# Strassen-like input projection: signs turned so that weight sums only add, and two of four sums moved from GpSimd into accumulating transfers

## The reference

```python
hm = rmsnorm(x, norm_g[layer]) * (1 + scale[:, None]) + shift[:, None]
proj = h @ w_in                        # layer 0: (640, 1024) @ (1024, 6144)
u_a, z_a, b_b, c_b, v_b, z_b = jnp.split(proj, 6, axis=-1)
```

## Time and profile before

| | us |
|---|---|
| median of three runs | 1180.3 (1178.32 to 1180.64) |
| the profiled execution | 1179.51 |
| its span in the trace | 1177.7 |
| TensorE busy in the span | 1087.3 |
| VectorE busy | 917.2 |
| ScalarE busy | 563.0 |
| GpSimd busy | 350.2 |

### The profile page before, as it was taken

How to read it: one execution, slowest core, us unless ns; L and a number is a source line. 1 busy time by engine, 2 the same in 40 slices (tenths; PEclk the granted TensorE clock), 3 DMA queues, 4 the chain that set the end, 5 groups by cost and what they waited for, 6 DMA issues and landing times.

```text
span 1177.7 us, 19458 instructions
## 1 busy us (share of the span) xinstructions
PE 1087.3 (92%) x6931; PEld 1006.6 (85%) x6931; DVE 917.2 (78%) x1577; ACT 563.0 (48%) x1154; POOL 350.2 (30%) x451
## 2 busy tenths in 40 slices
PE   5898999988898899999899999999999999879997
PEld 3797989888888888788899999999999999867785
DVE  2689999999999989747869696969696978766444
ACT  5343333333333334335565666666656666565321
POOL 1322221233333221013033443443443444443001
PEclk9899999999999999999999999999999999989999
DMA  9624334333333376314234343434343424272702
GB/s 325 210 82 116 101 107 117 102 95 98 97 99 95 104 280 199 100 37 161 75 91 140 92 131 107 130 108 130 108 126 96 126 85 136 79 263 86 293 19 90
DMA packets 178854, 148.24 MB, mean 126 GB/s; under 512 B 7964, under 2 KB 157828, under 8 KB 178388
## 3 DMA queue, kind: packets, MB, share of 16 engines
q1 hardware_dynamic: 173476, 130.08, 35.7%
q0 software_dynamic: 4864, 16.83, 4.9%
q10 hardware_dynamic: 432, 0.21, 0.1%
HBM read 134.32 MB, written 12.78 MB: 125 GB/s over the span
## 4 chain that ended last, share of the span: by engine, by line
PE 30%; DVE 18%; ACT 9%; issue 5%; DMA 3%; POOL 1%; SPq 1%; DVEq 0%; ACTq 0%; POOLq 0%
PE PS L526 13%; PE PS L1730 9%; DVE big L1940 4%; DVE big L1917 3%; ACT big L1851 2%; ACT big L1863 2%; PE PS L1789 2%; DVE big L1282 2%; DVE w_lo L301 2%; ACT w_hi L295 1%; DMA big<-l_scr 1%; DMA big<-y_scr 1%; PE PS L1491 1%; DVE big L1964 1%; PE PS L1716 1%
## 5 line engine op out<-in xcount | busy, mean ns | idle before, releaser
L906 ACT ACTIVATE w_hi<-raw_w 128x512 fp32r<-128x512 f32 x154 | 89.6, 624 | 168.3 <-DVE raw_w L935 56.0
L856 PE MATMUL PS<-h_hi,w_hi 128*128 128x320 f32 x352 | 113.9, 324 | 26.5 <-DVE big L1217 12.6
L301 DVE TENSOR_TENSOR w_lo<-raw_w,w_hi 128x1024 fp32r<-128x1024 f32 x84 | 110.6, 1321 | 28.3 <-ACT w_hi L295 27.1
L911 DVE TENSOR_TENSOR w_lo<-raw_w,w_hi 128x512 fp32r<-128x512 f32 x154 | 121.2, 813 | 6.8 <-ACT w_hi L906 6.7
L1716 PE MATMUL PS<-h_hi,w_hi 128*128 128x320 f32 x480 | 118.3, 328 | 0.0
L856 PE MATMUL PS<-h_hi,w_lo 128*128 128x320 f32 x352 | 111.2, 316 | 0.0
L856 PE MATMUL PS<-h_lo,w_hi 128*128 128x320 f32 x352 | 111.0, 315 | 0.0
L1716 PE MATMUL PS<-h_hi,w_lo 128*128 128x320 f32 x480 | 109.4, 309 | 0.0
L1716 PE MATMUL PS<-h_lo,w_hi 128*128 128x320 f32 x480 | 109.3, 309 | 0.0
L295 ACT ACTIVATE w_hi<-raw_w 128x1024 fp32r<-128x1024 f32 x84 | 88.0, 1050 | 39.9 <-PE PS L526 33.5
L856 PEld LDWEIGHTS PS<-h_hi,w_hi 128*128 128x128 f32 x352 | 68.1, 193 | 34.0 <-DVE big L1217 15.9
(11 more groups left out here) (276 smaller groups left out, 3013.3 us busy)
## 6 DMA issues: line engine op xcount, KB each, us to landing
raw_w<-in_ssd_w_in_dram SPq DMA_DIRECT2D x48, 512.0 KB, 5.0
raw_w<-in_fc_w_in_dram SPq DMA_DIRECT2D x88, 256.0 KB, 3.0
big<-l_scr SPq DMA_DIRECT2D x40, 512.0 KB, 4.5
big<-in_w_mod_dram POOLq DMA_DIRECT2D x32, 512.0 KB, 3.9
big<-in_w_mod_dram SPq DMA_DIRECT2D x16, 512.0 KB, 8.2
raw_w<-in_fc_w_out_dram SPq DMA_DIRECT2D x16, 512.0 KB, 4.4
raw_w<-in_ssd_w_out_dram SPq DMA_DIRECT2D x16, 512.0 KB, 7.8
y_scr<-big SPq DMA_DIRECT2D x40, 128.0 KB, 1.8
```

The lines of the kernel that those rows point to most:

```text
L301: dve.tensor_tensor(w_lo[:, slot, :], raw_w[:, slot, :], w_hi[:, slot, :].bitcast(F32), ALU.subtract).then_inc(lo_ready, 1)
L856: mm = pe.matmul(PS[:, BANK[r], 0:HALF], w[:, ws], h, start=(kt == 0 and j == 0), stop=(kt == 3 and j == 2))
L906: act.activation(qhi[r], b22_raw[n % 2] if r == B22 else qraw[r], ACT.Copy).then_inc(hi_ready, 3 if (n, r) == (23, B22) else 1)
L911: dve.tensor_tensor(qlo[r], b22_raw[n % 2] if r == B22 else qraw[r], qhi[r].bitcast(F32), ALU.subtract).then_inc(lo_ready, 3 if (n, r) == ...
```

## The change

T1 and T3 become sums: T1 = B12 + B11, T3 = B12 + B22, T2 = B22 + T1, T4 = T2 + B21. To keep the results, the signs of the token sums S1 and S4 and of three combinations of products are turned.

B12 is now loaded twice by SyncE's queue, into T3's slot and into T1's slot. Then GpSimd waits for both and issues two transfers with `accum_op=add`, which read B11 and B22 again from device memory and add them onto these slots (the transfers read 256 KB each, in rows of 512 bytes). T2 and T4 are made on VectorE, one after the other, where T4 was made before; VectorE's T3 is gone. ScalarE's conversions of T1 and T3 wait for their transfers, those of T2 and T4 for VectorE, and that of B11 only for B11's own load. SyncE's queue holds five loads a pair: B11, B21, B22, B12 for T3, B12 for T1.

```diff
@@ -271,7 +271,7 @@
         lfb_landed = [sem(f"lfb_landed{i}") for i in range(2)]
 
         half_landed = [sem(f"half_landed{k}") for k in range(2)]
-        w_sums, v_sums = sem("w_sums"), sem("v_sums")
+        t1_summed, t3_summed, t_landed, v_sums = sem("t1_summed"), sem("t3_summed"), sem("t_landed"), sem("v_sums")
         s_done, s_hi = sem("s_done"), sem("s_hi")
         modw_landed = [sem(f"modw_landed{t}") for t in range(2)]
         p1_copied, combined, gates_done = sem("p1_copied"), sem("combined"), sem("gates_done")
@@ -891,7 +891,7 @@
 
         def quarter_wait(eng, n, q):
 
-            eng.wait_ge(half_landed[q % 2], 32 * (n - 1))
+            eng.wait_ge(half_landed[q % 2], (16, 32)[q % 2] * (n - 1))
 
         def part_hi(act, n, r):
 
@@ -901,8 +901,10 @@
                 act.wait_ge(unit_used, pair_base(n - 1) + r + 1)
             if r in (B11, B21, B22):
                 quarter_wait(act, n, {B11: 0, B21: 1, B22: 3}[r])
+            elif r in (T1, T3):
+                act.wait_ge(t1_summed if r == T1 else t3_summed, 16 * (n - 1))
             else:
-                act.wait_ge(w_sums if r in (T1, T2) else v_sums, 2 * (n - 2) + {T1: 1, T2: 2, T4: 1, T3: 2}[r])
+                act.wait_ge(v_sums, 2 * (n - 2) + {T2: 1, T4: 2}[r])
             act.activation(qhi[r], b22_raw[n % 2] if r == B22 else qraw[r], ACT.Copy).then_inc(hi_ready, 3 if (n, r) == (23, B22) else 1)
 
         def part_lo(dve, n, r):
@@ -913,26 +915,20 @@
 
         def weights_pool(pool, n):
 
-            quarter_wait(pool, n, 0)
-            if n == 2:
-                pool.wait_ge(lo_ready, 3)
-            else:
-                pool.wait_ge(lo_ready, pair_base(n - 1) + T1 + 1)
-            pool.tensor_tensor(qraw[T1], qraw[T3], qraw[B11], ALU.subtract).then_inc(w_sums, 1)
-            quarter_wait(pool, n, 1)
-            pool.wait_ge(w_sums, 2 * n - 3)
-            if n > 2:
-                pool.wait_ge(v_sums, 2 * n - 5)
-            pool.tensor_tensor(qraw[T2], b22_raw[n % 2], qraw[T1], ALU.subtract).then_inc(w_sums, 1)
-        def weights_t4_dve(dve, n):
-
-            dve.wait_ge(w_sums, 2 * n - 2)
+            pool.wait_ge(t_landed, 32 * (n - 1))
+            for slot, kt0, col, summed in ((T1, 0, PAIR_COLS[n][0], t1_summed), (T3, 4, PAIR_COLS[n][1], t3_summed)):
+                pool.dma_start(qraw[slot].rearrange("p (k n) -> p k n", n=P), fc_src[:, kt0:kt0 + 4, col:col + P],
+                               accum_op=ALU.add).then_inc(summed, 16)
+
+        def weights_dve(dve, n):
+
+            dve.wait_ge(t1_summed, 16 * (n - 1))
+            quarter_wait(dve, n, 1)
             if n > 2:
                 dve.wait_ge(lo_ready, pair_base(n - 1) + T4 + 1)
-            dve.tensor_tensor(qraw[T4], qraw[T2], qraw[B21], ALU.subtract).then_inc(v_sums, 1)
-
-        def weights_t3_dve(dve, n):
-            dve.tensor_tensor(qraw[T3], b22_raw[n % 2], qraw[T3], ALU.subtract).then_inc(v_sums, 1)
+            dve.tensor_tensor(qraw[T2], b22_raw[n % 2], qraw[T1], ALU.add).then_inc(v_sums, 1)
+            dve.wait_ge(v_sums, 2 * n - 3)
+            dve.tensor_tensor(qraw[T4], qraw[T2], qraw[B21], ALU.add).then_inc(v_sums, 1)
 
         def pair_dst(n):
 
@@ -1113,7 +1109,7 @@
 
         def fourier_first_dve(dve):
             dve.wait_ge(v_done, 2 * KT)
-            dve.tensor_tensor(S1raw, xT0[:, 0:4, H1], xT0[:, 4:8, H1], ALU.add).then_inc(s_done, 1)
+            dve.tensor_tensor(S1raw, xT0[:, 0:4, H1], xT0[:, 4:8, H1], ALU.subtract).then_inc(s_done, 1)
             dve.wait_ge(act_freed, 1)
             fold_dve(dve, 0)
             dve.tensor_tensor(S3raw, xT0[:, 0:4, H0], xT0[:, 0:4, H1], ALU.subtract).then_inc(s_done, 1)
@@ -1122,11 +1118,10 @@
             dve.wait_ge(act_freed, 2)
             fold_dve(dve, 1)
             dve.wait_ge(s_done, 3)
-            dve.tensor_tensor(S4raw, xT0[:, 4:8, H0], S2raw, ALU.subtract).then_inc(s_done, 1)
+            dve.tensor_tensor(S4raw, xT0[:, 4:8, H0], S2raw, ALU.add).then_inc(s_done, 1)
             dve.wait_ge(s_done, 4)
             s_lo_dve(dve, 0)
-            weights_t4_dve(dve, 2)
-            weights_t3_dve(dve, 2)
+            weights_dve(dve, 2)
             s_lo_dve(dve, 1)
             part_lo(dve, 2, B11)
             part_lo(dve, 2, T2)
@@ -1202,19 +1197,18 @@
             if n in MOD_TILE and k not in ("v", "c"):
                 mod_tile_dve(dve, MOD_TILE[n])
             if n < 23:
-                weights_t4_dve(dve, n + 1)
+                weights_dve(dve, n + 1)
             dve.wait_ge(unit_used, base + T3 + 1)
             dve.wait_ge(combined, sums(n, U2))
             dve.tensor_tensor(u3, u2, PS[:, BANK[T3], 0:HALF], ALU.add).then_inc(combined, 1)
             if n < 23:
-                weights_t3_dve(dve, n + 1)
                 part_lo(dve, n + 1, T2)
             else:
                 y_split_dve(dve, 0, 0)
             dve.wait_ge(unit_used, base + T1 + 1)
             dve.wait_ge(combined, sums(n, U3))
-            dve.tensor_tensor(dst[:, 1, H1], PS[:, BANK[T1], 0:HALF], u3, ALU.add).then_inc(combined, 1)
-            dve.tensor_tensor(u2, PS[:, BANK[T1], 0:HALF], u2, ALU.add).then_inc(combined, 1)
+            dve.tensor_tensor(dst[:, 1, H1], PS[:, BANK[T1], 0:HALF], u3, ALU.subtract).then_inc(combined, 1)
+            dve.tensor_tensor(u2, PS[:, BANK[T1], 0:HALF], u2, ALU.subtract).then_inc(combined, 1)
             if n < 23:
                 part_lo(dve, n + 1, B21)
             else:
@@ -1222,7 +1216,7 @@
             if k == "b":
                 tap_left(dve, i, 1)
             dve.wait_ge(unit_used, base + T4 + 1)
-            dve.tensor_tensor(dst[:, 0, H1], u3, PS[:, BANK[T4], 0:HALF], ALU.subtract).then_inc(combined, 1)
+            dve.tensor_tensor(dst[:, 0, H1], u3, PS[:, BANK[T4], 0:HALF], ALU.add).then_inc(combined, 1)
             if k == "u":
                 dve.wait_ge(combined, sums(n, C21))
                 fold_dve(dve, 0)
@@ -2085,22 +2079,29 @@
 
         PAR_DMAS = 6
 
+        def quarter_load(sp, dst, kt0, col, landed_sem):
+
+            sp.dma_start(dst.rearrange("p (k n) -> p k n", n=P), fc_src[:, kt0:kt0 + 4, col:col + P]).then_inc(landed_sem, 16)
+
+        def slot_wait(sp, n, r):
+
+            sp.wait_ge(lo_ready, pair_base(n - 1) + r + 1 if n > 2 else r // 2 + 1)
+
         def quarter_loads(sp, n):
 
-            pair = PAIR_COLS[n]
-            for q, (slot, kt0, col) in enumerate(((0, 0, pair[0]), (2, 4, pair[0]), (3, 0, pair[1]), (6, 4, pair[1]))):
-                if n == 2:
-                    sp.wait_ge(lo_ready, slot // 2 + 1)
-                elif q < 3:
-                    sp.wait_ge(lo_ready, pair_base(n - 1) + slot + 1)
-                elif n == 3:
-                    sp.wait_ge(lo_ready, 4)
-                else:
-                    sp.wait_ge(lo_ready, pair_base(n - 2) + slot + 1)
-                if q != 2 and n > (3 if q == 3 else 2):
-                    sp.wait_ge(w_sums if q == 0 else v_sums, 2 * (n - 3) if q == 3 else 2 * (n - 3) + 1)
-                sp.dma_start((b22_raw[n % 2] if q == 3 else qraw[slot]).rearrange("p (k n) -> p k n", n=P),
-                             fc_src[:, kt0:kt0 + 4, col:col + P]).then_inc(half_landed[q % 2], 16)
+            left, right = PAIR_COLS[n]
+            slot_wait(sp, n, B11)
+            quarter_load(sp, qraw[B11], 0, left, half_landed[0])
+            slot_wait(sp, n, B21)
+            if n > 2:
+                sp.wait_ge(v_sums, 2 * (n - 2))
+            quarter_load(sp, qraw[B21], 4, left, half_landed[1])
+            sp.wait_ge(lo_ready, pair_base(n - 2) + B22 + 1 if n > 3 else 4)
+            quarter_load(sp, b22_raw[n % 2], 4, right, half_landed[1])
+            slot_wait(sp, n, T3)
+            quarter_load(sp, qraw[T3], 0, right, t_landed)
+            slot_wait(sp, n, T1)
+            quarter_load(sp, qraw[T1], 0, right, t_landed)
 
         def out_load(sp, layer, v):
 
@@ -2143,7 +2144,6 @@
             for n in PAIRS:
                 quarter_loads(sp, n)
 
-            sp.wait_ge(w_sums, 2 * len(PAIRS))
             sp.wait_ge(v_sums, 2 * len(PAIRS))
             for v in range(8):
                 sp.wait_ge(lo_ready, pair_base(23) + 2 * v + 2 if v < 3 else OUT0 + v - 3)
```

## The result

| | before | after |
|---|---|---|
| median of the runs on one chip, us | 1179.42 (4 runs) | 1197.76 (4 runs, 1195.87 to 1198.85) |
| ratio, 95% interval | | 1.0154 [1.0135, 1.0172] |
| span of the profiled execution | 1177.7 | 1195.4 |
| VectorE busy in it | 917.2 | 884.7 |

The kernel became 1.5% slower. The forecast was 0.5% slower, with 1183 to 1203 as its own range. The time lies in that range and the loop is there as forecast, but the rise is three times the forecast one, and its side is in part luck, as the account of the prediction shows. VectorE has 32.5 us less to do, what the forecast meant to free, and the time still grew.

The account below looks back on a forecast made before the run. VectorE, held up by GpSimd's sums, was taken to bound the stage of the pairs. Convolution +10.2 and Fourier -4.6 gave +5.6 on 1179.5, plus 0.8 for the runs' median: 1186 us; range 1160 to 1214, forecast's own 1183 to 1203.

Parts of the forecast that it names:

- Contention: VectorE and GpSimd hold each other up when both read operands; about 2.1 us per full interval, removed with GpSimd's sums.
- Rival 4: Issuing the accumulates contends as the sums did, so VectorE gets no relief: +18 us, 1199; chance 0.05.
- The loop: Stage of the pairs: next sums can't start before Y + 3.6 + X; intervals sum to +10.2 convolution, -4.6 Fourier.
- X: Accumulating transfer's time to landing: 6.0 us (3.6 + 1.9 + 0.5); each us worth 17 us, balance at 5.7.
- Y: VectorE's time from L932 to the end of the L911 freeing T1's slot: 5.3 to 6.9 us.
- the doubling: Within X: the add reads its destination as well as its source, so 0.95 us of packets becomes 1.9.
- The start: Stage's first pair: L932 at 66.9 comes late enough for the chain; costed at nothing, 2 us at most.
- The gate intervals: Three Fourier intervals of 20.3 us, to be set by VectorE's new work of 18.2 each: -6.3 us together.
- Rival 1: The transfer is quick, X from 3.6 to 5: 1161 us at 4.5, 1150 at 3.6; chance 0.36.
- Rival 2: X between 5.4 and 5.8, so gain and loss cancel: 1180 us; chance 0.10.
- Rival 3: The transfer is slow, X = 8, with T3 late as well: 1220 us, 1253 at the upper bound; chance 0.11.
- Removing ScalarE's wait: B11's conversion no longer waits for the third quarter; VectorE once idled 2.02 us for it; worth nothing in the sum.

Follow-up runs that it names:

- e12: e2 plus GpSimd making two sums per pair in an unused area that nobody waits for, and its wait for the loads: 1179.5 us, 0.9998 of before.
- e1: Changed kernel with the accumulates of 19 pairs issued into an unused area and nobody waiting for them: 1162.0 us, 0.9837 of before.
- e2: Changed kernel with the accumulating transfers left out altogether: 1153.5 us, 0.9786 of before.
- e7: Changed kernel with the first two modulation weight loads cut to a quarter of their columns: 1193.4 us.
- e4: Changed kernel with a second buffer for T1 and T3 in odd pairs except pair 9, and B12 loaded first: 1162.5 us, 0.9852 of before.
- e11: e4 with buffers shifted so pair 10 has new slots, pair 2's B12 first, pair 3's loads and accumulates before the modulation loads: 1151.7 us, 0.9763 of before.
- e8: Changed kernel with half of the matmuls of the Fourier branch's DFT left out: 1190.3 us.
- e9: e4 with the second buffer for pair 9 too, and pair 3's loads and accumulates ahead of the first modulation loads: 1158.7 us, 0.9821 of before.
- e3: Changed kernel with T3's accumulating transfer issued ahead of T1's: 1232.0 us, 1.0448 of before.
- e10: Kernel before, with ScalarE's conversion of B11 waiting only for B11's own quarter: 1179.8 us, 0.9997 of before.
- e5: Kernel before with only the signs turned, so all four weight sums are adds: 1179.3 us, 1.0003 of before.

## Why the prediction was right or wrong

**Contention: right.** L913 is at 683 ns and L1276 at 1277, as the prediction's test asked, and e12 prices the old contention: 17.5 us for the sums (against e1), 26 with the late branch-B product (against e2). An issue of an accumulate takes GpSimd 1.3 to 1.9 us, over twice the 0.57 I used, and yet the longest L913 of the stage has 706 ns: issues do not hold VectorE. Rival 4 is refuted. The Trainium skill (SBUF — State Buffer, the section on the two separate sides) says that a reading GpSimd instruction and a VectorE instruction with two SBUF inputs exclude each other; e1, e2 and e12 agree with it.

**The loop: right in kind, with two errors that cancel.** X is 4.9, not 6.0; from the free slot to the issue it is 4.2, not 3.6; together 9.1 (8.2 to 9.9, and 11.2 once, in pair 13) against 9.6. Y is 5.4, 6.4, 6.3 and 7.1 where I had 5.3, 5.3, 6.2 and 6.9. The convolution intervals are then 14.5 to 16.7, and that part was to give +10.2 and gave +12.2. In the 14 turns there and the two of the Fourier part that hang on the loop, load and transfer are 6.1 us shorter in all than I had them, and Y is 7.9 us longer. Where Y is 6.4, three of the four turns have a cause that I had waved off: the branch-B product doesn't end while VectorE waits, but holds the T2 sum itself, for 1.5 to 1.7 us instead of 0.69:
```profile
323.42 4.16 POOL L1322 TENSOR_TENSOR big<-big 128x640 f32<-128x640 f32 x2
```
```profile
326.67 1.47 DVE L929 TENSOR_TENSOR raw_w<-raw_w 128x512 f32<-128x512 f32 x1 [2.57 <-DMA raw_w<-in_fc_w_in_dram]
```
Inside X the packet was well placed: 34.3% of 16 engines over 380 us, less what the queue took before (12.1% of 16 x 360), over the accumulates' 23232 packets (26880 less 3648) are 60 ns, against 29 of a plain one: the doubling. 33 of them are 2.0 us; what was too long is the rest, 2.9 where I had 3.6 + 0.5. The Trainium skill ("Collectives: The Full Stack", the bandwidth ceiling) has the same factor, from the two sources that a reduction reads. Its "DMA: Bandwidth & Descriptors" (anatomy of a DMA on the GpSimd path) has a fit from which I estimate 2.6 us for the whole transfer; 4.9 are measured, so that fit does not serve here.

**The step that failed: the intervals and the start that do not hang on the loop.** The prediction named what would disprove it: intervals that lengthen while X is under 5. That came. The loop is still what I thought, since every T2 sum of the convolution part starts as its transfer lands; the sign points to the other terms. Of +17.7 us in the span the forecast had +5.6; the 12.1 missing are

- 4.1 at the start ("I cost it at nothing, and at 2 us at most").
- 4.7 in the Fourier part, forecast -4.6, measured +0.1 ("18.2 for the 20.3 ones").
- 2.0 in the convolution part (Y, above), and 1.3 after the last W.

The start, in order of time, VectorE and then GpSimd:
```profile
86.70 2.48 DVE L1276 SCALAR_TENSOR_TENSOR big<-big,cond 128x1024 f32<-128x1024 f32 x2 [2.53 <-DMA big<-in_w_mod_dram]
...
93.58 0.69 DVE L929 TENSOR_TENSOR raw_w<-raw_w 128x512 f32<-128x512 f32 x1 [4.40 <-DMA raw_w<-in_fc_w_in_dram]
```
```profile
79.14 1.12 POOL L1315 DMA_DIRECT2D big<-in_w_mod_dram  x2
...
88.78 2.66 POOL L920 DMA_DIRECT2D raw_w<-in_fc_w_in_dram  x2 [8.53 <-DMA raw_w<-in_fc_w_in_dram]
```
I had looked at pair 2 alone. Pair 3's two loads of B12 were issued at 78.9 and 79.4, beside two modulation loads of 512 KB, and landed at 85.7 and 88.5, after 6.8 and 9.1 us, where the stage's median is 3.3; only then could the accumulates start. (Before, a quarter load at this place took 7.9 us too, but what followed it was a sum of 1.6 us on GpSimd, not a transfer of 4.8.) e7 took three quarters of the bytes of these two modulation loads away and won 2.8 us from the first modulation load to W. e4, where the B12 loads need not wait for the slot, shows that the place in the queue counts as well: there pair 3's accumulates are issued at 81.67 and 82.46, right behind the modulation loads, and land after 9.6 and 11.0 us.
```profile
81.67 2.72 POOL L928 DMA_DIRECT2D big<-in_fc_w_in_dram  x2
```
```profile
93.45 0.69 DVE L937 TENSOR_TENSOR raw_w<-raw_w,big 128x512 f32<-128x512 f32 x1 [3.74 <-DMA big<-in_fc_w_in_dram]
```
So the second buffer alone wins little at the start: 12.9 us from the first modulation load to W, against 14.4 after. e11, with loads and accumulates ahead of the modulation loads, issues them at 72.99 and needs 8.5 us, less than before's 10.2. The share of each other load beside them was not tried.

The gate intervals: the first and the third are 19.1 us after, and all three are 19.1 in e2, without any accumulate. So it isn't the loop; the floor of 18.2 was wrong. The first two of them in e2:
```profile
103.40:122.50 19.10, 16.19 (x108) 14.93 (x107) 17.30 (x33) 7.58 (x17) 2.08 (x4) 1.00 0.52 152
137.20:156.30 19.10, 18.99 (x129) 18.07 (x129) 17.30 (x33) 7.80 (x17) 1.61 (x3) 1.00 0.48 140
```
VectorE is busy 17.30 us, 1.83 less than before, near the 2.1 that I took off, but it idles 1.8: the wait for ScalarE's step of the DFT (1.1) and for TensorE's products (0.6). I took the 20.3 of before as work less contention, and it had waits of its own that stay or grow. For TensorE I had counted the 84 matmuls of a pair and left out the DFT's 60 (30 in the code, each recorded twice). In the second row, where fewer records are missing, TensorE is busy 18.99 of 19.10 us: it is full there. That TensorE sets the 19.1 is read from this and not shown, since e8, which was to show it, got a lower clock. The miss is 0.9 us, three times.

The second gate interval after is 20.8. It contains a lower clock:
```profile
144.90:165.80 20.90, 19.21 (x118) 17.95 (x118) 17.56 (x33) 7.68 (x17) 3.71 (x4) 0.92 0.72 172
```
e11 shows the same two lengths in its first and second gate interval, one at 0.92 and one at 1.00:
```profile
103.30:124.00 20.70, 17.79 (x108) 16.53 (x107) 17.41 (x33) 7.57 (x17) 7.54 (x8) 0.92 0.82 179
...
138.70:157.80 19.10, 18.98 (x129) 18.07 (x129) 17.30 (x33) 7.80 (x17) 6.96 (x7) 1.00 0.73 170
```
So 1.7 us go with the clock; e1 and e4 have the same pair of lengths, though e9 has 20.1 at 0.92. Why the clock is lower in that interval stays open. The remaining 0.3 are loop turns slightly longer than forecast.

**Luck.** With the measured X the prediction's own sum gives a faster kernel: 17 x 1.1 less than its 1186 is 1167 us, and with the 4.2 from slot to issue as well, 17 x 0.5 less, it is 1177. So "slower", and a time inside 1183 to 1203, came from a loop taken half a microsecond too long per turn and from misses elsewhere that add up to more than the whole forecast rise.

**Rivals.** Rival 1, the quick transfer, was right on X (3.6 to 5) and wrong on the time: at 4.5 it gave 1161. Its sum used the same floors, and its 3.6 us from slot to issue was 4.2. Rival 2 (X at 5.4 to 5.8) wasn't met. Rival 3 is refuted as a forecast (X = 8), though e3 shows its slope. Removing ScalarE's wait was rightly put at nothing (e10), the signs too (e5).

## What to carry to other kernels

A transfer that makes an operand must start from a slot that is free early: the same accumulates cost 18 us with one buffer and won 28 with two and an earlier first turn, with no work removed. Price a chain from the moment its buffer comes free, and take each interval's floor from all that every engine does in it, waits included, not from its old length less the cost that goes. The first turn of a loop has other neighbours in the queues than the steady ones and needs its own look. And when a forecast hangs on a balance (here X = 5.7), small terms put at nothing can decide its side.

## What was not expected of the hardware

- GpSimd's instruction that issues an accumulate of 512 rows of 512 bytes takes 1.26 to 1.87 us, where the modulation loads' took 0.53 to 0.60 before. Plain issues behind one grow too, up to 1.68 us, and the 512 KB loads land in 6.4 us instead of 3.9; in e11, where few stand right behind one, they land in 4.1.
- Accumulates issued right behind two 512 KB loads took 9.6 and 11.0 us to land (e4), against 4.9 and 6.2 in the median after.
- The branch-B product held a residual for 4.86 us instead of 0.68 (e1), more than any instruction of the earlier trace rows was held.
- Where TensorE waits for the loop the granted clock falls: 0.94 over the stage (0.99 in e11), and 0.77 from 312.10 to 326.70.
